# Conditioned hybrid decoder layer on one core: the last gate's modulation in two runs, the expert weights' parts in another buffer, the ending shared by three engines

## The chip, the cores and the metric

The kernel runs on one core of a Trainium2 chip. The metric is the device time of one launch in microseconds (us). A profile is one further execution, recorded instruction by instruction; its times are counted from the start of its span.

## The reference, cut to what matters

Everything is float32. A prompt of 256 tokens and 8 sample sequences of 4 tokens (together T = 288 token columns, TP = 256 and TS = 32) pass through one layer. The layer's conditioning gives six modulation vectors per sequence; the last is `gate2`.

```
shift1, scale1, gate1, shift2, scale2, gate2 = split(silu(c) @ w_ada + b_ada)
h = rms_norm(x) * (1 + scale1) + shift1
... projections, sparse attention, conformer convolution, merge ...
x = x + gate1 * (merged @ w_out)
h2 = rms_norm(x) * (1 + scale2) + shift2
x = x + gate2 * peer(h2)

def peer(h):                      # 16384 experts, a row of u_emb and of v_emb each
    q = h @ w_q_peer              # 8 heads, two halves of 128
    pick 16 experts per head and token, softmax gates
    act = gelu(u_emb[picked] . h)
    return sum(gate * act * v_emb[picked])
```

## The kernel before, in words

The expert tables are not gathered for the prompt. All 16384 experts are computed densely in NSUB = 128 chunks of 128 experts: first `scores` for every chunk (u_emb chunk times h2, then gelu, stored to DRAM), later `outputs` for every chunk (v_emb chunk times the gated activations, summed in the eight PSUM banks `ps0` to `ps7`, one for each 128 output features). Only the 32 sample tokens gather their rows of v_emb, by indirect DMAs on POOL. To keep float32 accuracy at the speed of the rounded format, every weight tile and every right-hand side is cut into a high and a low part: ScalarE (ACT) copies the high part, POOL or VectorE (DVE) subtracts it for the low part, and TensorE (PE) multiplies high by high, high by low and low by high.

There is no scheduler. Each engine has its own instruction list, written out by hand or in hardware loops (`Fori`), and the lists are tied by counting semaphores (`wait_ge`). Each engine works its list strictly in order. SyncE (SP) issues the loads of the weight tiles into a ring of R = 4 slots.

Three places matter here.

**The last gate's modulation.** The tiles of w_ada for `gate2` come late. PE runs `late_ada(i, s, j)` for i in 0, 1: four float32 matmuls of 32x128 output each. It stands where PE would otherwise wait: behind the sums of squares of the second RMSNorm (`sums`, L1770), while ACT takes the root (L777), DVE the reciprocal (L1505), and h2 is made (DVE L1513, ACT L999 for the high part, DVE L1516 and L1520 for the low part). The half with i = 0 has two filler matmuls (`keep_busy`, L2120) behind each call; the half with i = 1 stands between the eight high-by-high matmuls of the first tile of the expert queries (`linear_cut(("peer_q", 0))`: L1832 high by high, L1842 high by low, L1848 low by high).

**From the last scores to the first outputs.** `scores` is L2171, L2172 and L2178 on PE, gelu is L1065 on ACT, the cut of a tile L1009 on ACT. The gated activations of a chunk are themselves cut: ACT L1103 makes the high part, DVE L1678 the low part, in a buffer `wr` that lies over the right-hand side of `scores`:

```
wr = rhs_parts[:, :, :]...            # the right-hand side of scores
...
eng.wait_ge(u_done, NSUB)             # ACT, ahead of the first high part of wr
...
pe.wait_ge(gelued, NSUB)              # PE, ahead of the first outputs
```

`outputs` is L2228 (high tile by both parts of `wr`, 512 columns) and L2231 (low tile by high part). DVE L1684 makes the low part of a v_emb tile.

**The ending.** The last `outputs` finishes the banks one after the other (`bank_done`). DVE adds `gate2` times the two halves of each bank to x: `first_half` (L1739) and `second_half` (L1744) for k = 0 to 7. Behind bank 4 PE multiplies the summed rows of the sample tokens (`samples`, L2256), which must wait until bank 0 has been read (`y_out` of 1) since they go into it; DVE scales and adds them (L1754, L1759). SP stores y in two DMAs of four chunks each (L638).

## Time and profile before

| | |
|---|---|
| median of 3 runs | 1251.37 us (1250.25 to 1252.94) |
| the profiled execution | 1250.7 us |
| its span | 1248.9 us |
| mean granted TensorE clock | 0.995 |
| PE busy | 1207.5 us (97% of the span) |
| DVE busy | 921.9 us (74%) |
| ACT busy | 592.2 us (47%) |
| POOL busy | 616.6 us (49%) |

Busy time of PE is modelled, since matmuls are pipelined: overlapping matmuls count once. PEld is the weight load of a matmul, which runs beside the matmul before it. Idle time of an engine that nobody waits for costs nothing. The profiled execution took 1.8 us more than its span, which lies outside of what the records show.

### The profile page before, as it was taken

To read this page: it belongs to the slowest core of one execution; us is meant where nothing else is said; L and a number is where in the kernel's file an instruction comes from. 1 tells how busy PE (TensorE), PEld (TensorE's weight loads), DVE (VectorE), ACT (ScalarE), POOL (GpSimd) and SP (SyncE) were. 2 spreads that over 40 slices of the span, in tenths; PEclk is the share of its full clock that TensorE was granted. 3 is DMA by queue.
4 is the path that set the end of the run, shared out by engine and by line. 5 is a ranking of instruction groups with operands and counts; after the bars stand their busy time and mean duration, and the time that the engine had idled before them with its cause. 6 is when DMAs were issued, how large, how long until landed. Compare 5 with 4: busy or idle time off the path is not lost.

```text
span 1248.9 us, 28196 instructions
## 1 busy us (share of the span) xinstructions
PE 1207.5 (97%) x8837; PEld 1114.8 (89%) x8837; DVE 921.9 (74%) x2247; ACT 592.2 (47%) x1015; POOL 616.6 (49%) x307
## 2 busy tenths in 40 slices
PE   5999999989999999999999999999999999999997
PEld 3887877989979999999999999999888888888886
DVE  4779985966754999959999998000567888888866
ACT  2332445657443445445554545444455455554452
POOL 0664564521755667766666666777203434434100
PEclk9999999999999999999999999999999999999999
DMA  9986555423743356655555555667767898888763
GB/s 361 318 268 223 166 199 186 140 86 120 262 151 135 125 188 207 214 186 188 185 180 183 182 179 186 205 207 246 255 232 284 308 345 290 309 310 309 275 225 125
DMA packets 113995, 273.12 MB, mean 219 GB/s; under 512 B 30928, under 2 KB 54192, under 8 KB 113552
## 3 DMA queue, kind: packets, MB, share of 16 engines
q1 hardware_dynamic: 105920, 248.96, 58.7%
q0 software_dynamic: 6432, 19.71, 4.4%
q10 hardware_dynamic: 1584, 3.68, 0.8%
q8 instruction: 34, 0.56, 0.2%
q14 instruction: 25, 0.20, 0.1%
HBM read 249.30 MB, written 23.00 MB: 218 GB/s over the span
## 4 chain that ended last, share of the span: by engine, by line
PE 82%; DVE 10%; DMA 2%; issue 1%; SPq 1%; ACT 1%; POOL 1%; ACTq 0%; DVEq 0%; POOLq 0%
PE ps L2228 19%; PE ps L2171 11%; PE ps L2178 11%; PE ps L2172 11%; PE ps L2231 10%; DVE ps L1212 6%; PE ps L1832 5%; PE ps L1848 5%; PE ps L1842 5%; PE ps L2207 2%; DMA ring<-in_stream 2%; DVE big L1231 1%; DVE big L1228 1%; PE ps L2148 1%; SPq L557 1%
## 5 line engine op out<-in xcount | busy, mean ns | idle before, releaser
L728 POOL TENSOR_TENSOR split<-ring,split 128x1024 fp32r<-128x1024 f32 x128 | 307.4, 2402 | 138.6 <-ACT split L1009 138.6
L1009 ACT ACTIVATE split<-ring 128x1024 fp32r<-128x1024 f32 x256 | 271.6, 1061 | 174.5 <-PE ps L2228 171.5
L668 POOL TENSOR_TENSOR split<-ring,split 128x1024 fp32r<-128x1024 f32 x76 | 186.8, 2463 | 190.5 <-ACT split L828 190.5
L2171 PE MATMUL ps<-h2r,split 128*128 128x288 f32 x1024 | 278.7, 297 | 0.7 <-ACT big L1035 0.5
L2172 PE MATMUL ps<-h2r,split 128*128 128x288 f32 x1024 | 279.0, 296 | 0.0
L2228 PE MATMUL ps<-h2r,split 128*128 128x512 f32 x1024 | 257.4, 392 | 1.4 <-DVE h2r L1678 1.4
L2228 PEld LDWEIGHTS ps<-h2r,split 128*128 128x128 f32 x1024 | 184.2, 189 | 34.5 <-issue 1.6
L2171 PEld LDWEIGHTS ps<-h2r,split 128*128 128x128 f32 x1024 | 192.9, 188 | 1.2 <-ACT big L1035 0.8
L2172 PEld LDWEIGHTS ps<-h2r,split 128*128 128x128 f32 x1024 | 192.4, 188 | 0.0
L2178 PE MATMUL ps<-h2r,split 128*128 128x288 f32 x1024 | 156.5, 295 | 0.0
L1684 DVE TENSOR_TENSOR split<-ring,split 128x1024 fp32r<-128x1024 f32 x128 | 156.1, 1219 | 0.0
L1065 ACT ACTIVATE act<-ps 128x288 f32<-128x288 f32 x124 | 51.0, 412 | 219.4 <-PE ps L2178 216.5
L741 POOL DMA_INDIRECT big<-in_stream,pick_at x32 | 62.8, 1962 | 175.6 <-DVE big L1698 127.9
L2231 PEld LDWEIGHTS ps<-h2r,split 128*128 128x128 f32 x1024 | 140.0, 190 | 9.9
L2231 PE MATMUL ps<-h2r,split 128*128 128x256 f32 x1024 | 143.8, 282 | 0.0
L2178 PEld LDWEIGHTS ps<-h2r,split 128*128 128x128 f32 x1024 | 141.4, 188 | 0.3 <-POOL split L728 0.3
L1637 DVE SCALAR_TENSOR_TENSOR hot<-ps,parts 128x256 fp32r<-128x256 f32 x256 | 124.2, 485 | 0.0
L828 ACT ACTIVATE split<-ring 128x1024 fp32r<-128x1024 f32 x84 | 88.6, 1055 | 62.9 <-DMA ring<-in_stream 52.0
L1212 DVE SCALAR_TENSOR_TENSOR ps<-big,ps 128x256 f32<-128x256 f32 x232 | 97.1, 485 | 2.0
L1636 DVE TENSOR_SCALAR hot<-ps,parts 128x128 fp32r<-128x128 f32 x256 | 90.0, 352 | 11.2 <-PE ps L2207 11.2
L1832 PE MATMUL ps<-h2r,split 128*128 128x288 f32 x544 | 89.8, 306 | 3.8 <-ACT split L828 3.7
L1832 PEld LDWEIGHTS ps<-h2r,split 128*128 128x128 f32 x544 | 76.5, 190 | 14.7 <-issue 9.7
(290 smaller groups left out, 1619.8 us busy)
## 6 DMA issues: line engine op xcount, KB each, us to landing
ring<-in_stream SPq DMA_DIRECT2D x371, 512.0 KB
act_dram<-act SPq DMA_DIRECT2D x128, 128.0 KB, 1.8
big<-in_stream SPq DMA_DIRECT2D x20, 512.0 KB, 7.6
parts<-act_dram SPq DMA_DIRECT2D x16, 512.0 KB
big<-act_dram SPq DMA_DIRECT2D x16, 512.0 KB, 5.2
big<-in_cache_k SPq DMA_DIRECT2D x16, 128.0 KB, 2.6
big<-in_cache_v SPq DMA_DIRECT2D x16, 128.0 KB, 3.0
s_act_dram<-act SPq DMA_DIRECT2D x128, 16.0 KB, 1.5
```

Of the source, the lines that this page charges most:

```text
L668: nc.gpsimd.tensor_tensor(split[:, n % 2, 1], ring[:, POS[CUT[n]] % R, :], split[:, n % 2, 0].bitcast(f32), ALU.subtract).then_inc(lin_lo, 1)
L728: nc.gpsimd.tensor_tensor(split[:, n % 2, 1], ring[:, slot_of(n), :], split[:, n % 2, 0].bitcast(f32), ALU.subtract).then_inc(lo_ready, 1)
L1009: nc.scalar.activation(split[:, n % 2, 0], ring[:, slot_of(n), :], ACT.Copy).then_inc(hi_ready, 1)
L1212: ins = V.scalar_tensor_tensor(acc if j < CW - 1 else y[:, k, 0:TP], zp[:, k, j:j + TP], w, acc, ALU.mult, ALU.add)
L1637: return V.scalar_tensor_tensor(hot1[:, slot], iota_ps.unsqueeze(1).to_broadcast([P, 2, P]), parts[:, 0, col], parts[:, 2:4, col].to_broad ...
L1684: V.tensor_tensor(split[:, n % 2, 1], ring[:, slot_of(n), :], split[:, n % 2, 0].bitcast(f32), ALU.subtract).then_inc(lo_ready, 1)
L1832: MM(out, hi[:, k], rhs_h[:, k], start=(k == 0), stop=False)
L2171: MM(out, u_hi[:, k], h_hi[:, k], start=(k == 0), stop=False)
L2172: last = MM(out, u_hi[:, k], h_lo[:, k], start=False, stop=False)
L2178: last = MM(out, u_lo[:, k], h_hi[:, k], start=False, stop=(k == KC - 1))
L2228: return MM(ps[k][:, 0:2 * TP], v[0][:, k], w_both, start=first, stop=last)
L2231: return MM(ps[k][:, 0:TP], v[1][:, k], wr[:, n % 2, 0], start=False, stop=False)
```

## The change

It does three things, and none of them changes what is computed.

1. The two halves of `late_ada` run one behind the other with four fillers between them, ahead of the first tile of the expert queries, whose matmuls stand alone again.
2. `wr` lies over the one-hot rows (`hot1`), which are no longer used by then. So ACT makes the first high part behind the third last chunk's place in the gelu list, `behind` the gelu of chunk 126, and PE starts the first outputs with banks 2 to 7; it waits for the last gelu only ahead of banks 0 and 1, which the scores used. DVE's first low tile waits for the last scores where it waited for those before.
3. At the end the second halves of k = 1, 3 and 5 are scaled by ACT into `y_low` and added by POOL, and the sample tokens' tail is copied out of PSUM by ACT and scaled and added by POOL. DVE waits for ACT to have read a shared bank before it reads it. SP stores y in five DMAs: four of two chunks' prompt columns, and one of all sample columns.

```diff
-        wr = rhs_parts[:, :, :].rearrange("p a n -> p (a n)")[:, 0:4 * TP].rearrange("p (s a t) -> p s a t", a=2, t=TP)
+        wr = hot1[:, :, :, :].rearrange("p n a i -> p (n a i)").rearrange("p (s a t) -> p s a t", a=2, t=TP)
+        SHARED = (1, 3, 5)
+        y_low = parts[:, 0:len(SHARED)]
@@ sync
-            sp.wait_ge(s_scaled, 2)
-            for half in range(2):
-                ks = slice(half * KC // 2, (half + 1) * KC // 2)
-                sp.wait_ge(y_out, ks.stop)
-                sp.dma_start(a["yT"][:, ks], ye[:, ks]).then_inc(stored, 16)
-            sp.wait_ge(stored, 16 * 6)
+            for k in range(0, KC, 2):
+                sp.wait_ge(y_out, sum(n not in SHARED for n in range(k + 2)))
+                sp.wait_ge(y_odd, sum(n < k + 2 for n in SHARED))
+                if k == KC - 2:
+                    sp.wait_ge(s_scaled, 2)
+                    sp.dma_start(a["yT"][:, :, TP:T], ye[:, :, TP:T]).then_inc(stored, 16)
+                sp.dma_start(a["yT"][:, k:k + 2, 0:TP], ye[:, k:k + 2, 0:TP]).then_inc(stored, 16)
+            sp.wait_ge(stored, 16 * 9)
@@ gpsimd, at its end
+            pool.wait_ge(x_loaded, 16)
+            for i, k in enumerate(SHARED):
+                pool.wait_ge(y_scaled, i + 1)
+                pool.wait_ge(y_half, k + 1)
+                nc.gpsimd.tensor_tensor(ye[:, k, 0:TP], ye[:, k, 0:TP], y_low[:, i], ALU.add).then_inc(y_odd, 1)
+                if i == 1:
+                    pool.wait_ge(s_unfolded, 1)
+                    picked = dtmp.rearrange("p (k b t) -> p k b t", b=NSEQ, t=TD)
+                    nc.gpsimd.tensor_tensor(picked, picked, gate2[:, :, 1:NG].unsqueeze(3).to_broadcast([P, KC, NSEQ, TD]),
+                                            ALU.mult).then_inc(s_scaled, 1)
+                    pool.wait_ge(s_scaled, 1)
+                    nc.gpsimd.tensor_tensor(ye[:, :, TP:T], dtmp.rearrange("p (k c) -> p k c", c=TS), xe[:, :, TP:T],
+                                            ALU.add).then_inc(s_scaled, 1)
@@ scalar
-            with eng.Fori((BEFORE + MIXED) // R, NSUB // R) as g:
+            with eng.Fori((BEFORE + MIXED) // R, NSUB // R - 1) as g:
                 turn(g, False)
+            def high_weights(g, b, n, first=False):
+                eng.wait_ge(weighted, g * R + (n + 1))
+                if not first:
+                    eng.wait_ge(o_done, g * R + (n - 1))
+                nc.scalar.activation(wr[:, n % 2, 0], act_bs[b][:, n], ACT.Copy).then_inc(w_hi, 1)
+            turn(NSUB // R - 1, False, lambda: high_weights(0, 0, 0, True), R - 2)
...
+            for i, k in enumerate(SHARED):
+                eng.wait_ge(bank_done, k + 1)
+                nc.scalar.activation(y_low[:, i], ps[k][:, TP:2 * TP], ACT.Copy, scale=gate2[:, k, 0:1]).then_inc(y_scaled, 1)
+                if i == 1:
+                    eng.wait_ge(s_folded, 1)
+                    nc.scalar.activation(dtmp, ps[0][:, 0:KC * TS], ACT.Copy).then_inc(s_unfolded, 1)
@@ vector
-                    value_low(c, n, *((u_done, NSUB - 1 + i) if first and i < 2 else (o_done, c - 1)))
+                    value_low(c, n, *((u_done, NSUB) if first and i < 2 else (o_done, c - 1)))
...
                 if k + 1 < KC:
+                    if k + 1 in SHARED:
+                        dve.wait_ge(y_scaled, SHARED.index(k + 1) + 1)
                     first_half(k + 1)
-                second_half(k)
-                if k == 4:
-                    dve.wait_ge(s_folded, 1)
...
+                if k not in SHARED:
+                    second_half(k)
@@ tensor
-            for s in range(R):
-                for j in range(2):
-                    late_ada(0, s, j)
-                    keep_busy(2)
+            for i in range(2):
+                for s in range(R):
+                    for j in range(2):
+                        late_ada(i, s, j)
+                if i == 0:
+                    keep_busy(4)
...
-                linear_cut(("peer_q", n), between=(lambda k: late_ada(1, k // 2, k % 2)) if n == 0 else None)
+                linear_cut(("peer_q", n))
...
-                for k in range(KC):
+                for k in (*range(2, KC), 0, 1) if first else range(KC):
+                    if first and k == 0:
+                        pe.wait_ge(gelued, NSUB)
                     ins = high(k)
...
-            pe.wait_ge(gelued, NSUB)
```

On PE, from the sums of squares (L1770) into the first expert query tile. `ps5` and `ps6` take the two halves of the modulation, `ps7` the fillers, `ps0` the query tile. Before:

```order
L1770 MATMUL ps3<-big,ones 128x288 x2
L1875 MATMUL ps5<-big 32x128 x4
L2120 MATMUL ps7<-y_r 128x288 x2
L1875 MATMUL ps5<-big 32x128 x4
L2120 MATMUL ps7<-y_r 128x288 x2
...
L1832 MATMUL ps0<-h2r,split 128x288
L1875 MATMUL ps6<-big 32x128 x4
L1832 MATMUL ps0<-h2r,split 128x288
L1875 MATMUL ps6<-big 32x128 x4
...
L1842 MATMUL ps0<-h2r,split 128x288 x8
L1848 MATMUL ps0<-h2r,split 128x288 x8
```

And in the changed kernel, where the same functions stand at L1803 (`sums`), L1906 (`late_ada`), L2151 (filler) and L1865, L1873, L1879 (the three products):

```order
L2151 MATMUL ps7<-y_r 128x288 x6
L1803 MATMUL ps3<-big,ones 128x288 x2
L1906 MATMUL ps5<-big 32x128 x32
L2151 MATMUL ps7<-y_r 128x288 x4
L1906 MATMUL ps6<-big 32x128 x32
L1865 MATMUL ps0<-h2r,split 128x288 x8
L1873 MATMUL ps0<-h2r,split 128x288 x8
L1879 MATMUL ps0<-h2r,split 128x288 x8
```

The second half has moved ahead of the query tile, and 12 of 16 fillers are gone.

On ACT of the changed kernel, the last four chunks' gelus (L1089), the cuts of tiles (L1033) and the high parts of `wr` (L1126), which before all stood behind the last gelu:

```order
L1033 ACTIVATE split<-ring 128x1024
L1089 ACTIVATE act<-ps0 128x288
L1126 ACTIVATE hot1<-parts 128x256
L1033 ACTIVATE split<-ring 128x1024
L1089 ACTIVATE act<-ps1 128x288
L1033 ACTIVATE split<-ring 128x1024
L1126 ACTIVATE hot1<-parts 128x256
```

The first high part stands ahead of the cut of tile 128 and of the last gelu; the second stands where it stood.

On DVE at the very end, before (L1739 is a first half, L1744 a second half, `psN` the bank):

```order
L1739 SCALAR_TENSOR_TENSOR big<-ps0,gate2,big 128x256
L1739 SCALAR_TENSOR_TENSOR big<-ps1,gate2,big 128x256
L1744 SCALAR_TENSOR_TENSOR big<-ps0,gate2,big 128x256
...
L1739 SCALAR_TENSOR_TENSOR big<-ps5,gate2,big 128x256
L1744 SCALAR_TENSOR_TENSOR big<-ps4,gate2,big 128x256
L1754 TENSOR_TENSOR big<-ps0,gate2 128x256
L1759 TENSOR_TENSOR big<-big 128x8x32
L1739 SCALAR_TENSOR_TENSOR big<-ps6,gate2,big 128x256
L1744 SCALAR_TENSOR_TENSOR big<-ps5,gate2,big 128x256
L1739 SCALAR_TENSOR_TENSOR big<-ps7,gate2,big 128x256
L1744 SCALAR_TENSOR_TENSOR big<-ps6,gate2,big 128x256
L1744 SCALAR_TENSOR_TENSOR big<-ps7,gate2,big 128x256
```

And in the changed kernel (L1777 a first half, L1782 a second half):

```order
L1777 SCALAR_TENSOR_TENSOR big<-ps0,gate2,big 128x256
L1777 SCALAR_TENSOR_TENSOR big<-ps1,gate2,big 128x256
L1782 SCALAR_TENSOR_TENSOR big<-ps0,gate2,big 128x256
...
L1777 SCALAR_TENSOR_TENSOR big<-ps4,gate2,big 128x256
L1777 SCALAR_TENSOR_TENSOR big<-ps5,gate2,big 128x256
L1782 SCALAR_TENSOR_TENSOR big<-ps4,gate2,big 128x256
L1777 SCALAR_TENSOR_TENSOR big<-ps6,gate2,big 128x256
L1777 SCALAR_TENSOR_TENSOR big<-ps7,gate2,big 128x256
L1782 SCALAR_TENSOR_TENSOR big<-ps6,gate2,big 128x256
L1782 SCALAR_TENSOR_TENSOR big<-ps7,gate2,big 128x256
```

Three second halves and the two instructions of the sample tokens are gone from the list; the first halves of `ps1`, `ps3` and `ps5` each wait for ACT.

## Rows read from the trace of the kernel before

**Rows 1.** The page: busy time, share of the span, instructions by engine.

```profile
PE 1207.5 (97%) x8837; PEld 1114.8 (89%) x8837; DVE 921.9 (74%) x2247; ACT 592.2 (47%) x1015; POOL 616.6 (49%) x307
```

**Rows 2.** Waits of PE from 377 to 1243, largest first: us, times, longest.

```profile
PE ps L2148 <- ACT big L818: 2.0, 4, 0.5
PE ps L2228 <- DVE h2r L1678: 1.4, 1, 1.4
...
```

**Rows 3.** Timeline around the modulation: start, length, instruction, idle before it.

```profile
361.95 1.21 PE L1770 MATMUL ps<-big,ones 128*128 128x288 f32 x4 [0.69 <-DVE big L1492]
363.08 0.43 PE L1875 MATMUL ps<-big 128*32 128x128 f32 x8
367.03 3.31 ACT L999 ACTIVATE h2r<-big,mod 128x256 fp32r<-128x256 f32 x8
...
369.99 3.25 DVE L1520 SCALAR_TENSOR_TENSOR h2r<-big,mod,h2r 128x256 fp32r<-128x256 f32 x8
376.07 1.22 PE L1848 MATMUL ps<-h2r,split 128*128 128x288 f32 x8
```

**Rows 4.** Timeline: long runs of the same 32-wide matmuls early in the kernel.

```profile
16.54 3.64 PE L1864 MATMUL ps<-big 128*32 128x128 f32 x64
21.11 1.52 PE L1864 MATMUL ps<-big 128*32 128x128 f32 x48
```

**Rows 5.** Stretches, PE alone: length, PE busy (matmuls), granted clock, DMA share, GB/s.

```profile
178.00:181.40 3.40, 1.95 (x14) 0.99 0.89 292
181.50:184.50 3.00, 3.00 (x14) 0.50 0.03 11
369.40:374.90 5.50, 5.50 (x74) 1.00 0.00 1
```

**Rows 6.** Timeline from the last scores to the first outputs.

```profile
881.43 0.41 ACT L1065 ACTIVATE act<-ps 128x288 f32<-128x288 f32 x1 [1.76 <-PE ps L2178]
881.74 0.41 ACT L1103 ACTIVATE h2r<-parts 128x256 fp32r<-128x256 f32 x1
882.18 0.43 DVE L1678 TENSOR_TENSOR h2r<-parts,h2r 128x256 fp32r<-128x256 f32 x1 [18.93 <-ACT h2r L1103]
882.75 2.06 PE L2228 MATMUL ps<-h2r,split 128*128 128x512 f32 x8 [1.36 <-DVE h2r L1678]
882.85 1.22 DVE L1684 TENSOR_TENSOR split<-ring,split 128x1024 fp32r<-128x1024 f32 x1
890.49 1.06 ACT L1009 ACTIVATE split<-ring 128x1024 fp32r<-128x1024 f32 x1 [1.41 <-DMA ring<-in_stream]
893.98 2.00 PE L2228 MATMUL ps<-h2r,split 128*128 128x512 f32 x8
```

**Rows 7.** Timeline of the ending.

```profile
1238.19 0.88 DVE L1739 SCALAR_TENSOR_TENSOR big<-ps,gate,big 128x256 f32<-128x256 f32 x2 [1.14 <-PE ps L2228]
1239.60 1.94 PE L2256 MATMUL ps<-fold,big 128*128 128x32 f32 x16
...
1242.02 0.48 DVE L1739 SCALAR_TENSOR_TENSOR big<-ps,gate,big 128x256 f32<-128x256 f32 x1 [0.21 <-PE ps L2228]
...
1244.78 0.87 DVE L1744 SCALAR_TENSOR_TENSOR big<-ps,gate,big 128x256 f32<-128x256 f32 x2
1245.67 0.35 SPq L638 DMA_DIRECT2D out_yT<-big  x1
```

**Rows 8.** Nearest rows for the new operations; DMAs: KB each, us to landing.

```profile
L682 POOL TENSOR_TENSOR big<-big 128x256 f32<-128x256 f32 x7 | 5.2, 739 | 0.8 <-POOL big L682 0.5
L1040 ACT ACTIVATE big<-ps 128x256 f32<-128x256 f32 x1 | 0.4, 383 | 0.0
act_dram<-act SPq DMA_DIRECT2D x128, 128.0 KB, 1.8
s_act_dram<-act SPq DMA_DIRECT2D x128, 16.0 KB, 1.5
out_yT<-big SPq DMA_DIRECT2D x2, 576.0 KB, 2.8
```

More of the change, by code:

```diff
@@ L425, in build @@
         y_half = sem("y_half")
+        y_scaled = sem("y_scaled")
+        y_odd = sem("y_odd")
+        s_unfolded = sem("s_unfolded")
         s_scaled = sem("s_scaled")
@@ L1055, in _, with turn @@
                 gelu(c, c, c < 2)
-            def turn(g, tokens4, behind_first=None):
+            def turn(g, tokens4, behind=None, at=0):
                 for n in range(R):
@@ L1065, in turn @@
                     nc.scalar.activation(act[:, n % 2], ps[n % 2][:, 0:T], ACT.Gelu_apprx_tanh).then_inc(gelued, 1)
-                    if behind_first and n == 0:
-                        behind_first()
+                    if behind and n == at:
+                        behind()
                     if tokens4:
@@ L1093, in _ @@
                 turn(g, True)
-            with eng.Fori((BEFORE + MIXED) // R, NSUB // R) as g:
+            with eng.Fori((BEFORE + MIXED) // R, NSUB // R - 1) as g:
                 turn(g, False)
+            def high_weights(g, b, n, first=False):
[4 more added lines that the diff above has]
+            turn(NSUB // R - 1, False, lambda: high_weights(0, 0, 0, True), R - 2)
             def v_turn(g, b, first=False, last=False):
                 for n in range(R):
-                    eng.wait_ge(weighted, g * R + (n + 1))
-                    if not first or n >= 2:
-                        eng.wait_ge(o_done, g * R + (n - 1))
-                    nc.scalar.activation(wr[:, n % 2, 0], act_bs[b][:, n], ACT.Copy).then_inc(w_hi, 1)
+                    if not first or n:
+                        high_weights(g, b, n, first and n < 2)
                     m = (n + 1) % R
@@ L1749, in _ @@
                 if k + 1 < KC:
+                    if k + 1 in SHARED:
+                        dve.wait_ge(y_scaled, SHARED.index(k + 1) + 1)
                     first_half(k + 1)
-                second_half(k)
-                if k == 4:
-                    dve.wait_ge(s_folded, 1)
-                    V.tensor_tensor(dtmp.rearrange("p (k b t) -> p k b t", b=NSEQ, t=TD),
-                                    ps[0][:, 0:KC * TS].rearrange("p (k b t) -> p k b t", b=NSEQ, t=TD),
-                                    gate2[:, :, 1:NG].unsqueeze(3).to_broadcast([P, KC, NSEQ, TD]), ALU.mult)\
-                        .then_inc(s_scaled, 1)
-                    dve.wait_ge(s_scaled, 1)
-                    V.tensor_tensor(ye[:, :, TP:T], dtmp.rearrange("p (k c) -> p k c", c=TS), xe[:, :, TP:T], ALU.add)\
-                        .then_inc(s_scaled, 1)
+                if k not in SHARED:
+                    second_half(k)
         @block.tensor
@@ L1812, in _, with linear_cut @@
             g_hi, g_lo = (rhs_other[:, part].rearrange("p (k t) -> p k t", t=T) for part in range(2))
-            def linear_cut(key, *halves, between=None):
+            def linear_cut(key, *halves):
                 n = CUT.index(key)
@@ L1832, in linear_cut @@
                             MM(out, hi[:, k], rhs_h[:, k], start=(k == 0), stop=False)
-                            if between:
-                                between(k)
                     if key == ("peer_q", 0) and half == 0:
```

## The prediction

> **What bounds the kernel now.** I read the profile's page first: PE is busy 97% of the span, every other engine 74% or less [rows 1]. Then all waits of PE from 377 us to the ending: four of 0.5 us in which it waits for ACT's copy of a query tile (L2148), and one of 1.4 us ahead of the first outputs; what is left out is shorter still [rows 2]. So between 377 and 1243 us nothing but PE's own work takes time: if PE gets to 377 earlier, the end comes earlier by as much. The places where PE doesn't work at full density are those that the change touches: the thin stretch before 377 us, the 1.4 us before the first outputs, and the ending, where DVE and a store come last. I read the timeline of the three, one after the other.
>
> **Part 1, the modulation.** It adds no work and takes 12 fillers away. What matters is which chain lets the third product of the first query tile (low by high) start, and at what time. It starts at 376.07 and takes 1.22 [rows 3]. Behind the sums, which end at 361.95 + 1.21 = 363.16, PE now has 32 float32 matmuls, four fillers, 32 matmuls. In the trace a float32 matmul shows as two rows, so each run is 64 rows. 48 such rows took 1.52 us, which makes 2.0 for 64; another run of 64 took 3.64 [rows 4]. Fillers go by the dense 128x288 matmul, 1.22 / 8 = 0.15 each [rows 3]. PE reaches the query tile at 363.16 + 2.0 + 0.6 + 2.0 = 367.8 at the best, at 371.0 at the worst. There it meets two chains that don't change: ACT makes the eight high pieces of h2 from 367.03, the last at 370.34; DVE makes the low pieces from 369.99, the last at 369.99 + 3.25 = 373.24 [rows 3]. Even from 371.0, eight high-by-high matmuls are done at 372.2. So DVE comes last in both cases, and the low-by-high product starts at about 373.4 instead of 376.07: **−2.6 us**. Before, PE reached that point later than DVE, because eight late_ada calls stood between. The cuts and copies behind this tile (ACT, POOL) were released by PE and move along.
>
> What it gives back is the clock. From 367.8 to 373.4 PE has 16 matmuls of 0.15, that is 2.4 us of work in 5.6 us. The interleaved calls kept it busy for 5.50 of 5.50 us there, at a granted clock of 1.00 [rows 5]. Elsewhere, after a stretch of 3.40 us with 1.95 busy, the clock stood at 0.50 for the next 3.00 us [rows 5], the 1.2 GHz level. If it falls here, a stretch of such length costs at most half of it, 1.5 us, if it lies wholly in the dense work behind 373.4, and nothing if it lies wholly in the thin part. It should reach over both; I take **+1.0** of 0 to 1.5. (TensorE: Matmul & The Clock Gate of the Trainium skill, section "Why this matters for your kernels", warns of idle gaps between bursts. The gaps here are of 0.25 us between single matmuls, so by that rule there would be no fall and the term would be 0; the row at 178 us holds a gap of its own, so it doesn't tell the two apart.)
>
> **Part 2, the first outputs.** PE is free at 882.75 − 1.36 = 881.39, and waits for a chain that began with the last gelu: gelu 881.43, first high part 881.74, first low part 882.18 [rows 6]. Now the high part is made one gelu earlier and the low part follows on DVE, which had been idle for 18.93 us [rows 6]. Bank 0 waits for the last gelu, done at 881.84, but is now the seventh bank in the list, and each takes 2.06 / 8 = 0.26, so it is wanted 1.5 us after the start. The high tile by bank 2 can start at once. The DVE low part of the tile, 1.22 us from 882.85 before [rows 6], only waits for the last scores, so it comes at about 881.4 to 882.7, before the low-by-high product needs it at 881.4 + 2.1 = 883.5. I take the whole wait, **−1.4**. The lower bound of the gain is set further on. The tile whose cut ACT began at 890.49 was waited for as a transfer, and that transfer isn't made earlier, since SP issues it after a store that hangs on the last gelu. The cut ends at 891.55, the parts of the weights follow it (0.40 on ACT, 0.43 on DVE: 892.4), and PE used them at 893.98; now it wants them at 892.6 [rows 6]. That leaves 0.2 us. If the transfer or a neighbour slips by more, it eats the gain one for one. So 0 to 1.4.
>
> **Part 3, the ending.** DVE's list loses three second halves and two operations of the sample tokens, at about 0.4 us each. But the first half of bank 1 now waits for ACT's read of it: 0.38 [rows 8]. Two first halves took 0.88 from 1238.19 [rows 7], so the second started at about 1238.6; now 1239.0. The reading of bank 0 and so the sample matmuls slip from 1239.60 to about 1239.95, and bank 5 from 1242.02 to 1242.4 [rows 7]. ACT copies the folded samples first, then scales bank 5: the first half of 5 starts at about 1242.8. Behind it stand five halves 0.40 apart, the last 0.48 long: 1245.3, against 1244.78 + 0.87 = 1245.65 [rows 7]. POOL takes 0.74 for an operation of this size [rows 8]. Three of them from 1242.2 end at 1244.4, hidden by DVE with 0.8 to spare. SP then issues the sample columns and, 0.4 later, the last pair, at about 1245.7, no earlier than the last store before (1245.67, landing 2.8 later with 576 KB [rows 7, 8]). The last is 256 KB now; 128 KB landed after 1.8 [rows 8]. Between the two by size is 2.1; with three more stores close by I take 2.4. **−0.4**, of −0.7 to +0.8, the upper end if DVE's list or POOL's is longer by two operations.
>
> The term that no row shows is the store of the sample columns: 1024 rows of 128 B. The nearest is the store of 16 KB in rows of 128 B, which landed after 1.5, where 128 KB in rows of 1 KB took 1.8 [rows 8]. Small rows were not dear there, but there were only 8 for each of the 16 DMA engines; here there are 64. Below: 1.8, as for its size. Above: if all of the 1.5 us were row time, 64/8 x 1.5 = 12. I take it as hidden in the last store's 2.4. (DMA: Bandwidth & Descriptors of the Trainium skill, section "Specifications", wants 512 B or more for the line rate and has a read-modify-write below that, which speaks against this store; the pair of rows neither shows nor excludes it at this count.)
>
> **Sum.** −2.6 + 1.0 − 1.4 − 0.4 = −3.4. The profiled execution took 1250.7, 0.67 less than the median of the three runs, 1251.37. So 1247.3 for a run like the profiled one, and **1247.9** as median.
>
> **Rivals.**
> - **No fall of the clock** (22%). For: the matmuls never stop for longer than a fraction of a us. Against: the row at 0.50 after a stretch of similar density. 1246.9. (This is where the Trainium skill's rule on idle gaps, named above, would lead.)
> - **The wait before the first outputs comes back later** (10%), at the tile cut at 890.49, with 0.2 us of slack. Part 2 is worth nothing: 1249.3.
> - **The ending costs** (10%). ACT stands ahead of DVE three times, and each wait may be longer than the 0.38; POOL's three operations may be slower. +0.6 for −0.4: 1248.9.
> - **Part 1 pays nothing** (8%). The clock falls for longer, or more than once, or PE's first tile waits for something else at its new place, such as the low part of the next tile. 1250.5.
> - **Slower: the store of the sample columns** (6%). It is issued at about 1245.3, and all stores were landed at 1248.47 before. Without the ending the change gives −3.0, so it breaks even when that store takes 1248.47 + 3.0 − 1245.3 = 6.2 us, or 96 ns for a row on each engine. At the ceiling of 12 us the end is at 1257.3, 8.8 later than before: 1251.4 + 8.8 − 3.0 = 1257.2.
> - What is left, 44%, is the forecast, its own range 1247.2 to 1248.9.
>
> **How the numbers follow.** This kernel's runs lie 2.7 us apart, so I call 0.2% (2.5 us, 1248.9) the least that can be told from no change. Faster: the forecast less its upper edge (42%), no fall (22%), half of the costly ending (5%), together about 0.69. Same: the returned wait (10%), part 1 for nothing (8%), the other half of the ending (5%), and the edge (2%): 0.25. Slower: 0.06. The range goes from 1246.2 (no fall, and the ending at −0.7, less some scatter) to 1250.5; above it lie the slow rival and a part of the rival ahead, under 2 in 10 together.
>
> **What would show it.** In the profile after: low by high (L1879) of the first query tile starts within 0.3 us of 373.4, right behind DVE's last low piece; the granted clock between 371 and 377 tells forecast from first rival. No idle before the first L2261, and none behind it that names a DMA or ACT near 892. DVE's first half of bank 5 waits for ACT and the last second half ends near 1245.3 minus what PE gained; the last two stores land within 3 us of their issue. A PE that waits for POOL at the second query tile, a cut near 890 that still waits for its transfer while PE waits for the cut, or a store of the samples that lands after the last pair would each make it wrong.

## The result, and the profile after

The changed kernel takes 1254.96 us (median of 10 runs, 1252.68 to 1257.52), the kernel before 1250.28 in the 10 runs beside it. The ratio is 1.0032, 95% interval 1.002 to 1.0045: slower by about 4 us, where 3.4 less was forecast. The profiled execution took 1255.31 us, its span 1253.4.

The page of the changed kernel: busy time by engine, and the granted clock in 40 slices.

```profile
PE 1212.0 (97%) x8825; PEld 1117.6 (89%) x8825; DVE 917.5 (73%) x2242; ACT 595.3 (47%) x1019; POOL 605.1 (48%) x312
PEclk9999999899999999999999999999999999999998
```

PE is still busy 97% of the time, and 12 matmuls fewer take 4.5 us more than in [rows 1]. A page alone doesn't tell why. What does is to cut both traces at the same five events and to compare the stretches:

| stretch, us | before | after | difference |
|---|---|---|---|
| start to the first matmul of the second norm's sums | 361.95 | 363.25 | +1.30 |
| from there to the second query tile | 15.18 | 13.54 | −1.64 |
| to the first scores | 61.91 | 61.90 | −0.01 |
| to the first outputs | 443.71 | 442.19 | −1.52 |
| to DVE's first read of bank 0 | 355.44 | 359.70 | +4.26 |
| to the end of the span | 10.71 | 12.84 | +2.13 |

DVE's first read of bank 0 is the first `first_half`, where the ending begins. The first line lies ahead of the change and is taken up with the experiments. The second and fourth are parts 1 and 2 of the prediction, near what it said. The fifth and the sixth are the loss.

**The modulation.** Timeline of the changed kernel (start, length, instruction, idle before it), and PE in stretches (length, busy, granted clock, DMA share, GB/s):

```profile
363.25 1.21 PE L1803 MATMUL ps<-big,ones 128*128 128x288 f32 x4 [0.68 <-DVE big L1530]
364.39 1.95 PE L1906 MATMUL ps<-big 128*32 128x128 f32 x64
366.27 0.79 PE L2151 MATMUL ps<-y_r 128*128 128x288 f32 x4
366.99 1.96 PE L1906 MATMUL ps<-big 128*32 128x128 f32 x64
368.99 3.10 PE L1865 MATMUL ps<-h2r,split 128*128 128x288 f32 x8
...
371.29 3.25 DVE L1558 SCALAR_TENSOR_TENSOR h2r<-big,mod,h2r 128x256 fp32r<-128x256 f32 x8
...
375.01 1.95 PE L1879 MATMUL ps<-h2r,split 128*128 128x288 f32 x8
376.79 1.22 PE L1865 MATMUL ps<-h2r,split 128*128 128x288 f32 x8
```

```profile
371.40:373.20 1.80, 1.80 (x6) 1.00 0.02 5
373.20:376.60 3.40, 3.40 (x12) 0.50 0.02 5
376.60:380.00 3.40, 3.40 (x28) 1.00 0.46 154
```

Both runs of 64 rows took 1.96 us, and low by high starts 11.76 us behind the sums' first matmul, 14.12 before [rows 3]. In the second half of the thin stretch the clock falls to 1.2 GHz, and the eight matmuls from 375.01 take 1.95 us for 1.22.

**The first outputs.** In the changed kernel PE goes from the last scores to the first outputs without idle time (the wait of 1.36 us in [rows 6] is gone):

```profile
879.81 1.23 PE L2211 MATMUL ps<-h2r,split 128*128 128x288 f32 x8
880.88 2.02 PE L2261 MATMUL ps<-hot,split 128*128 128x512 f32 x8
```

**The outputs.** Both kernels at the same place, 120 us into the outputs. Before:

```profile
1000.13 2.00 PE L2228 MATMUL ps<-h2r,split 128*128 128x512 f32 x8
1001.97 1.11 PE L2231 MATMUL ps<-h2r,split 128*128 128x256 f32 x8
1002.92 0.86 PE L2228 MATMUL ps<-h2r,split 128*128 128x512 f32 x3
```

After:

```profile
999.69 2.03 PE L2261 MATMUL ps<-hot,split 128*128 128x512 f32 x8
1001.55 1.12 PE L2264 MATMUL ps<-hot,split 128*128 128x256 f32 x8
1002.51 0.86 PE L2261 MATMUL ps<-hot,split 128*128 128x512 f32 x3
```

The sixteen matmuls of a chunk are called a group here: eight 128x512 of the high tile (the high product) and eight 128x256 of the low tile (the low product). The starts are to be read, not the lengths: from one group to the next it is 2.79 us before and 2.82 after. Over all groups the medians are 2.793 and 2.827; from the sixth on they scatter by about 1 ns (standard deviation). PE waits for nobody in either once the first group has started. 126 intervals at 0.034 make the 4.3 us. The only thing that changed in these matmuls is where `wr` lies.

**The ending.** The changed kernel:

```profile
1240.58 0.48 DVE L1777 SCALAR_TENSOR_TENSOR big<-ps,gate,big 128x256 f32<-128x256 f32 x1 [1.18 <-PE ps L2261]
...
1241.37 0.48 DVE L1777 SCALAR_TENSOR_TENSOR big<-ps,gate,big 128x256 f32<-128x256 f32 x1 [0.31 <-ACT parts L1151]
...
1245.32 0.48 DVE L1777 SCALAR_TENSOR_TENSOR big<-ps,gate,big 128x256 f32<-128x256 f32 x1 [1.51 <-ACT parts L1151]
...
1246.24 0.73 POOL L781 TENSOR_TENSOR big<-big,parts 128x256 f32<-128x256 f32 x1
1246.89 0.87 DVE L1782 SCALAR_TENSOR_TENSOR big<-ps,gate,big 128x256 f32<-128x256 f32 x2
1247.79 0.60 SPq L647 DMA_DIRECT2D out_yT<-big  x1
1248.44 0.65 SPq L648 DMA_DIRECT2D out_yT<-big  x1
```

DVE is done 7.18 us behind its first read of bank 0 (7.46 before, [rows 7]), the stores landed at 1251.18 by the raw records, and the span ends at 1253.4. In the raw records each engine closes the program with a `DRAIN`, which no view lists, and the one that ends last is POOL's; the span ends 0.24 us behind it. Its records (start us, length ns):

```
before   POOL DRAIN 1163.206 11817     last landing 1248.50   span 1248.89
after    POOL DRAIN 1245.915  7265     last landing 1251.18   span 1253.42
```

### The profile page after: what moved, and what is told of

It reads as the page before. It is cut to its first block, busy times and chain, and to the rows that moved or that the text cites. A ratio compares the mean times of both kernels' runs of the same rounds, so it can differ in the third digit from the quotient of the medians.

```text
span 1253.4 us, 28179 instructions
## 1 busy us (share of the span) xinstructions
PE 1212.0 (97%) x8825; PEld 1117.6 (89%) x8825; DVE 917.5 (73%) x2242; ACT 595.3 (47%) x1019; POOL 605.1 (48%) x312
## 4 chain that ended last, share of the span: by engine, by line
PE 83%; DVE 10%; DMA 3%; issue 1%; SPq 1%; ACT 1%; POOL 1%; DVEq 0%; ACTq 0%; POOLq 0%
PE ps L2261 19%; PE ps L2204 11%; PE ps L2211 11%; PE ps L2205 11%; PE ps L2264 10%; DVE ps L1250 6%; PE ps L1865 5%; PE ps L1879 5%; PE ps L1873 5%; DMA ring<-in_stream 3%; PE ps L2240 2%; DVE big L1269 1%; DVE big L1266 1%; PE ps L2181 1%; SPq L564 1%
## 5 line engine op out<-in xcount | busy, mean ns | idle before, releaser
L1033 ACT ACTIVATE split<-ring 128x1024 fp32r<-128x1024 f32 x256 | 271.4, 1060 | 176.5 <-PE ps L2261 168.4
L2261 PE MATMUL ps<-hot,split 128*128 128x512 f32 x1024 | 260.6, 395 | 0.0
L2261 PEld LDWEIGHTS ps<-hot,split 128*128 128x128 f32 x1024 | 183.7, 188 | 35.1
L2204 PEld LDWEIGHTS ps<-h2r,split 128*128 128x128 f32 x1024 | 192.9, 188 | 1.2 <-ACT big L1059 0.8
L2205 PEld LDWEIGHTS ps<-h2r,split 128*128 128x128 f32 x1024 | 192.5, 188 | 0.0
L1089 ACT ACTIVATE act<-ps 128x288 f32<-128x288 f32 x124 | 51.2, 413 | 219.1 <-PE ps L2211 216.4
L2264 PEld LDWEIGHTS ps<-hot,split 128*128 128x128 f32 x1024 | 140.6, 188 | 11.7
L751 POOL DMA_INDIRECT big<-in_stream,pick_at x32 | 52.7, 1646 | 190.3 <-DVE big L1736 143.6
L2264 PE MATMUL ps<-hot,split 128*128 128x256 f32 x1024 | 144.5, 282 | 0.0
L2211 PEld LDWEIGHTS ps<-h2r,split 128*128 128x128 f32 x1024 | 141.5, 188 | 0.3 <-POOL split L738 0.3
L1865 PE MATMUL ps<-h2r,split 128*128 128x288 f32 x544 | 90.7, 308 | 3.1 <-ACT split L852 2.9
L1865 PEld LDWEIGHTS ps<-h2r,split 128*128 128x128 f32 x544 | 77.3, 192 | 14.4 <-issue 7.4
```

The source lines that it names most:

```text
L1033: nc.scalar.activation(split[:, n % 2, 0], ring[:, slot_of(n), :], ACT.Copy).then_inc(hi_ready, 1)
L1865: MM(out, hi[:, k], rhs_h[:, k], start=(k == 0), stop=False)
L2204: MM(out, u_hi[:, k], h_hi[:, k], start=(k == 0), stop=False)
L2205: last = MM(out, u_hi[:, k], h_lo[:, k], start=False, stop=False)
L2211: last = MM(out, u_lo[:, k], h_hi[:, k], start=False, stop=(k == KC - 1))
L2261: return MM(ps[k][:, 0:2 * TP], v[0][:, k], w_both, start=first, stop=last)
```

## The experiments

One table holds all figures: the stretches of each profiled execution (us), and the ratio of its timed runs to those of the kernel before on the same chip. From the second query tile to the first scores all took 61.9 or 62.0 (e3 62.7, since its clock was still at half when the second tile began).

| run | to the sums | to query tile 2 | scores | outputs | ending | ratio [95%] |
|---|---|---|---|---|---|---|
| before | 361.95 | 15.18 | 443.71 | 355.44 | 10.71 | |
| after | 363.25 | 13.54 | 442.19 | 359.70 | 12.84 | 1.0032 [1.002, 1.0045] |
| e1 | 362.12 | 13.67 | 439.67 | 357.70 | 12.83 | 1.0003 [0.9986, 1.002] |
| e2 | 359.39 | 15.18 | 443.69 | 356.29 | 10.70 | 1.001 [0.9995, 1.0024] |
| e3 | 360.28 | 13.68 | 442.53 | 361.35 | 10.67 | 1.0015 [1.0, 1.0029] |
| e4 | 359.93 | 15.19 | 443.72 | 355.46 | 14.06 | 1.0044 [1.0029, 1.006] |
| e5 | 364.79 | 13.60 | 443.73 | 355.44 | 10.69 | 0.9999 [0.999, 1.0008] |
| e6 | 359.57 | 15.19 | 443.73 | 356.00 | 10.70 | one run |
| e7 | 359.62 | 15.18 | 443.69 | 358.85 | 10.70 | one run |
| e8 | 361.39 | 12.77 | 439.69 | 355.43 | 10.67 | 0.9961 [0.9948, 0.9975] |
| e9 | 364.06 | 12.77 | 443.77 | 355.45 | 10.69 | 0.9975 [0.9961, 0.999] |
| e10 | 365.13 | 15.20 | 443.71 | 355.45 | 11.27 | one run |
| e11 | 363.32 | 15.20 | 439.67 | 355.43 | 10.67 | 0.9967 [0.9954, 0.998] |
| e12 | 361.11 | 12.79 | 439.67 | 355.43 | 10.22 | 0.9942 [0.9921, 0.9963] |
| e13 | 361.52 | 13.66 | 441.81 | 357.47 | 12.85 | 1.0005 [0.9992, 1.0019] |
| e14 | 361.17 | 12.77 | 439.70 | 354.59 | 10.21 | 0.9945 [0.9932, 0.9959] |

**e1: `hot1` on a multiple of 64.** In both kernels `hot1` starts at byte 221920 of a partition, the old `wr` at 49280.

```diff
+        sb("pad", 8)
         hot1 = sb("hot1", NHOT, 2, P, dt=f32r)
```

> The changed kernel with eight unused words (32 bytes) ahead of hot1, so that wr starts at byte 221952 of a partition, a multiple of 64, and not at 221920, which is 32 past one. Nothing else. Theory 'start': the high tile's 128x512 product of the outputs reads wr in pieces of 64 bytes, and a start off such a piece costs one more piece for each matmul; the trace of the changed kernel has 2.83 us from one group of eight to the next in the outputs, before had 2.79. It expects 2.79 again, 4.3 us less over the 127 groups, so about 1250.7 by the changed kernel's median of 1255.0; perhaps 1 us less still, since the one-hot matmuls read hot1 too. Rival 'neighbour': hot1 is slower because it lies close to parts and the other small buffers that ACT and DVE write at the same time. It expects 2.83 and no change, 1255. Rival 'order': the outputs are slower since the weights' parts are made one step earlier; no change either.

The time came as expected, the stretches did not. The outputs gained 2.0, not 4.3: the two slots of `wr` take 2.821 and 2.799 us for a group, and two groups near 887, where ACT's cut waited for a transfer, were 0.1 longer. The scores gained 2.5, not 1. All of it lies in the part in which the one-hot matmuls run (231.14 us, 233.63 in the changed kernel); they read `hot1` and `hot2`, which the unused words both shift. A right total from two wrong terms; the start matters, but not in units of 64 bytes alone.

**e2: the kernel before with `wr` 32 bytes on.**

```diff
-... [:, 0:4 * TP].rearrange("p (s a t) -> p s a t", a=2, t=TP)
+... [:, 8:8 + 4 * TP].rearrange("p (s a t) -> p s a t", a=2, t=TP)
```

> The kernel before with one edit: wr starts 8 words (32 bytes) further into the right-hand side's buffer, so 32 bytes past a multiple of 64, and is read and written as before. Theory 'start': 2.83 us for each group of the outputs in place of 2.79, so about +4.3 us on the kernel before (ratio 1.0034), with the buffer, its neighbours and the order of before. Rivals 'neighbour' and 'order': no change, ratio 1.000.

A miss in size: 2.800 us for a group, +0.85 us in the outputs. The high product went from 1.841 to 1.867 as in the changed kernel, but the low one from 0.953 to 0.933. So a start alone changes both products, in either direction, and the first form of the theory (one more piece of 64 bytes) falls.

**e3: the changed kernel with the ending of before** (DVE, ACT, POOL and SP lists of the ending as before).

> The changed kernel with the ending of before: all halves and the sample tokens on DVE, nothing on ACT and POOL, two stores. From the first read of bank 0 to the end of the span the trace has 10.7 us before and 12.8 after. Theory 'drain': what closes the program on POOL (a drain of 7.3 us that the raw records show from 1245.9 to 1253.2 in the changed kernel, 6.2 us past POOL's last addition, and that lay hidden at 1163 to 1175 before) ends after all else. It expects 10.7 from bank 0 to the end again, and about 2.1 us less than the changed kernel: 1252.9. Rival 'stores': the five stores cost the 2.1 us; it expects the same here, and is told apart by e4. Rival of the prediction's sum: the shared ending saves, so taking it out costs 0.4: 1255.4.

The ending is 10.67 us again, and the median 1252.84. But other stretches of its profile differ too. The clock was at half for 6.8 us, so that the first part of the change gained 0.7 us up to the scores and not 1.6:

```profile
368.80:375.60 6.80, 6.80 (x24) 0.50 0.08 21
```

The outputs took 361.35, 1.65 more than in the changed kernel with the same `wr`. PE waited once, near 890, for the chain that starts with the load of a tile (us, times, longest):

```profile
PE ps L2242 <- DVE hot L1692: 1.5, 1, 1.5
```

**e4: the kernel before with a late instruction on POOL.**

```diff
                 gather_score(j)
+
+            pool.wait_ge(y_out, KC)
+            nc.gpsimd.memset(parts[:, 0, 0:4], 0.0)
```

> The kernel before with one added instruction on POOL: it waits until all eight banks are added on DVE (1245.65 in the trace before) and writes 4 words of a buffer that is no longer read. Nothing waits for it. Theory 'drain': POOL's closing then begins at about 1246 and takes 6 to 7 us past the added instruction, so the span ends at 1252.0 to 1252.6 and not at 1248.9: +3.1 to +3.7 us, ratio 1.0025 to 1.003. Rival 'stores' or any other in which POOL's closing costs nothing: the stores still end last, at 1248.5, and nothing changes.

Timeline of its last instructions:

```profile
1242.81 0.86 DVE L1747 SCALAR_TENSOR_TENSOR big<-ps,gate,big 128x256 f32<-128x256 f32 x2
1243.70 0.35 SPq L638 DMA_DIRECT2D out_yT<-big  x1
1243.73 0.10 POOL L768 MEMSET parts<- 128x4 f32 x1 [78.41 <-DVE big L1747]
```

Nobody waits for these 0.10 us, and the span ends 6.4 us behind them: POOL's `DRAIN` runs from 1243.71 for 6.32 us, the stores had landed at 1246.51. The ending is 3.35 us longer. The timed runs lose 0.29% to 0.6%, somewhat more than the trace's 0.27%.

**e5: the first part of the change alone**, on the kernel before.

> The kernel before with the first part of the change alone: both halves of the last gate's modulation in two runs with four fillers between, the first query tile's matmuls alone. The changed kernel and two variants of it all show the granted clock at half somewhere between 368 and 376 us. If the prediction's part 1 holds: low by high of the first query tile starts 11.8 us after the sums' first matmul (14.1 before), the clock falls to 0.50 for 3.4 us, and the second query tile starts 1.6 us earlier against the sums than before, so -1.6 us (ratio 0.9987). Rival 'no fall': -2.4. Rival 'pays nothing': 0. The outputs stay at 2.793 us for a group and the ending at 10.7.

The stretch and the fall came as forecast (0.50 from 374.9 to 378.3), −1.58 us. But the timed runs are equal to before, 0.9999, and 0.9987 lies just outside the interval. That asked for e9.

**e6 and e7: four starts in one run.** The kernel before, with `wr` in four slots. The edit of e6 is shown, with its starts in words; e7 has (24, 32, 152, 160):

```diff
+        WR = (0, 8, 4, 12)
+        flat = rhs_parts[:, :, :].rearrange("p a n -> p (a n)")
+        wrs = [flat[:, s * 4 * TP + o:s * 4 * TP + o + 2 * TP].rearrange("p (a t) -> p a t", t=TP) for s, o in enumerate(WR)]
```

> The kernel before with four slots for wr in place of two, one for each chunk of a group of four, each 4096 bytes on and with a start of its own: 0, 32, 16 and 48 bytes past a multiple of 64. So one run shows the time of a group of outputs matmuls at four starts. Theory 'start' in its first form (a piece of 64 bytes more): slot 0 as before, 2.793 us and 1.84 for its eight 128x512 matmuls, the other three alike, near 1.87. If it is the address in more bits than these, the pattern of the eight gaps within slot 1 is that of e2 (234 231 235 233 ns) only where its higher bits don't matter. Rival 'neighbour': all four alike at 2.793.

> As the run before, with starts 96, 128, 608 and 640 bytes past those of the kernel before (which is 128 past a multiple of 512). Slot 0 then agrees with the changed kernel's wr in the low nine bits of its address, slot 2 in the low twelve; slots 1 and 3 agree so with the wr of e1. Theory 'start': slots 0 and 2 take 2.827 and show the changed kernel's pattern of gaps in the high product (238 231 232 ns, repeated), slots 1 and 3 take about 2.80 to 2.82. Rival 'neighbour': wr lies in the old buffer, so all take 2.793.

Mean gaps between matmul starts over all 30 groups of a slot, worked out from the traces (ns; start of `wr` modulo 512 bytes; high and low are the sums over eight gaps):

```
run, slot      start  group  high  low    the eight gaps of the low product
before            128   2793  1841   952   113 119 120 120 120 120 120 120
e6 slot 0         128   2795  1846   949   117 118 119 121 117 118 120 120
e6 slot 2         144   2787  1853   933   114 119 114 119 114 119 114 119
e2, both          160   2800  1867   933   116 117 117 116 117 117 116 117
e6 slot 1         160   2803  1870   933   117 117 117 117 117 117 117 117
e6 slot 3         176   2802  1857   944   118 117 116 118 120 117 120 118
after, both       224   2827  1867   959   118 121 117 125 116 123 118 121
e7 slots 0, 2     224   2832  1873   959   118 121 117 125 116 124 118 121
e7 slots 1, 3     256   2808  1855   953   117 123 120 119 115 118 121 120
e1 slot 0         256   2821  1867   954   122 120 119 115 117 122 120 119
e1 slot 1         256   2799  1857   942   118 113 116 124 120 119 115 117
e13, both         128   2793  1841   953   114 119 120 120 120 120 120 120
e14, both         144   2787  1853   933   119 114 119 114 119 114 119 114
```

In e7 `wr` lies in the old buffer, written and read as before, and the outputs take 3.41 us more than before. Slots 0 and 2 have the changed kernel's gaps in the low product to 1 ns; in the high product the expected pattern did not come (227 236 233 235 232 240 233 237, where the changed kernel has 237 231 232 repeated), and a group takes 5 ns more. Slots 0 and 2 start 512 bytes apart (and two slots of 4096), as slots 1 and 3 do, and agree to the nanosecond. So the move to another buffer is not needed for the cost: the start counts, in bits below 512.

It is not all. The same start gives 2793 or 2795, 2800 or 2803 and 2827 or 2832, the second of each in a run whose other slots start elsewhere; that the slot ahead does it is a guess. And the two slots of e1 differ by 22 at one start. The weights' tile alternates between two places as the slots do. Where both slots have the same start (128, 144, 160 and 224) that makes no difference, at 256 in e1 it may; no run separates the two.

**e8: a candidate.** The changed kernel with `hot1` as in e1, the ending of before, `wr` over `hot1` for the first four chunks alone, a filler behind each matmul of the first two products of the first query tile, and SP's wait for the stored activations behind the first four loads of v_emb tiles:

```diff
+        def wr_of(c):
+            return wr_first if isinstance(c, int) and c < R else wr_later
...
+                            if key == ("peer_q", 0):
+                                keep_busy(1)
...
-            for s in range(2):
-                sp.wait_ge(act_stored[s], 32 * NSUB // 2)
...
             for n in range(R):
                 load_expert(NSUB + n, n)
+            for s in range(2):
+                sp.wait_ge(act_stored[s], 32 * NSUB // 2)
```

> A candidate that keeps what pays: the changed kernel with hot1 on a multiple of 64; wr over hot1 for the first four chunks alone and where it was before for the other 124; the ending of before; a filler behind each of the sixteen matmuls of the first query tile's first two products, to hold the clock; and SP's wait for the stored activations behind the first four loads of v_emb tiles, not ahead of them. By the traces so far, against before: modulation -2.4 (-1.6 if the clock falls in spite of the fillers), first outputs -1.4 and no wait for a tile between 885 and 893, one-hot products on an aligned buffer -2.3 (first outputs 503.6 us behind the first query tile's last product in e1, 505.9 in the changed kernel), outputs 2.793 for a group, ending 10.7. Sum -6.1: ratio 0.995. If the early loads collide with the stores that they now overtake, a wait comes back near 890 and it is -5.

0.9961, 1245.0 us against 1249.89. Its stretches are as expected (−6.5 us in sum where −6.1 was); the timed ratio says −4.9. Near 883 ACT now waits for PE and no longer for a transfer, and with the fillers the clock stays up (two views of e8):

```profile
883.48 1.06 ACT L1020 ACTIVATE split<-ring 128x1024 fp32r<-128x1024 f32 x1 [1.43 <-PE ps L2250]
```

```profile
367.10:369.50 2.40, 2.37 (x13) 1.00 0.00 0
369.50:374.80 5.30, 5.30 (x34) 1.00 0.02 5
```

**e9: the modulation with fillers, on the kernel before.**

> The kernel before with the first part of the change alone, and one filler behind each of the sixteen matmuls of the first query tile's first two products. The trace of the candidate shows that with them the clock stays up and the second query tile starts 12.8 us after the sums' first matmul (13.6 without fillers in e5, 15.2 before). If what lies between the sums and the end were all, this would be -2.4 us (ratio 0.998). e5 was timed equal to before (0.9999) where its stretch behind the sums gained 1.6. In all five traces with the new modulation the clock fell near 28 us, in the five without it once, and their sums start at 362.4 on average against 360.1. Theory 'start-up': something in the first 80 us is dearer in these programs by 1.5 to 2.5 us: then the ratio is 0.999 to 1.000 here too. Rival 'chance': the profiles fell so by chance, ratio 0.998.

0.9975, by its stretch 0.9981. So the modulation pays, and 'start-up' gets little support.

**e10: the kernel before with five stores.**

> The kernel before with its ending on DVE as it was, but y stored as in the changed kernel: four stores of two chunks' prompt columns and, ahead of the last, one of all sample columns in 1024 rows of 128 bytes. In the changed kernel the stores landed 3.4 us after DVE's last half (1247.76 to 1251.18), before 2.85 (1245.65 to 1248.50). If the stores cost what that says, the span's part from the first read of bank 0 is 11.3 here, against 10.7; the store of the sample columns takes 0.6 to issue and about 1.1 to move. The prediction's slower rival (96 ns and more for a row on each engine) expects 13 and more; its sum expects 10.3.

The ending is 11.27, 0.56 longer, as the changed kernel said. Rows of its end:

```profile
1248.00 0.87 DVE L1745 SCALAR_TENSOR_TENSOR big<-ps,gate,big 128x256 f32<-128x256 f32 x2
1248.90 0.60 SPq L638 DMA_DIRECT2D out_yT<-big  x1
1249.54 0.66 SPq L639 DMA_DIRECT2D out_yT<-big  x1
```

**e11: the candidate with the old modulation.**

> The candidate e8 with the modulation of before. By the traces its stretches are: first outputs -1.5 and one-hot products -2.5 in the scores, all else as before, so -4.0 us (ratio 0.9968). e8 was timed at 0.9961 where its stretches said -6.4 (0.9949). Theory 'start-up': the new modulation costs 1.5 to 2.5 us ahead of the sums, so that it gives 1 us at most in all, and this kernel comes out within 1 us of e8 (0.996 to 0.997). Rival 'chance': e8 is 2.4 us faster than this one.

0.9967, just what its own stretches say (−4.07 us). e10 and e11 have the old modulation and still come to the sums at 365.1 and 363.3, with the clock at half for 6.8 us from 27.5 and 25.7. So what differs ahead of the sums is not tied to the new modulation, and 'start-up' is dropped. Against e8 the ratio differs by 0.0006 where the stretches say 0.002; the intervals overlap and don't decide that.

**e12: the candidate with three stores** (four chunks, two and two, full rows).

```diff
+            for lo, end_k in ((0, 4), (4, 6), (6, 8)):
+                ks = slice(lo, end_k)
```

> The candidate e8 with y stored in three pieces of full rows, four chunks, two and two, so that the last store is 288 KB and not 576. In the trace of before the last store's rows move from about 1247.0 to 1248.2; with half of them that is about 0.6 to 0.8 less. Expected: 9.9 to 10.1 us from the first read of bank 0 to the end of the span, 10.7 before, and a ratio of 0.9955 (e8: 0.9961). If a store's length is mostly the time until its first row, the ending stays at 10.5 or more.

10.22, 0.45 less than e8, where 0.6 to 0.8 was forecast. At 0.9942 (1243.12 us against 1250.22) it is the fastest by median ratio.

**e13: `hot1` at the old start modulo 512.** The edit of e1 with 104 words in place of 8.

> The changed kernel with 104 unused words (416 bytes) ahead of hot1, so that wr starts at byte 222336, which is 128 past a multiple of 512, as the wr of the kernel before (49280) is. In e7, starts that agree in their low nine bits gave the same time in every slot, so theory 'low nine bits' expects here what before had, in the changed kernel's own buffer: 2.793 us for a group of outputs and 1.841 for its high product (233 236 228 232 231 227 227 227 ns), 355.5 us for the stretch of the outputs in place of 359.7, so 4.2 less than the changed kernel; and 1 to 2.5 us less in the scores, since the one-hot rows start there too. Against before: modulation -1.6, scores -4, outputs 0, ending +2.1: ratio 0.997. Rival 'buffer': e1, whose wr starts at 256 past a multiple of 512, had 2.821 and 2.799 in its two slots where e7 had 2.808 in the old buffer, so something of the buffer may matter as well; then 2.80 to 2.82 here. Early waits for tiles near 890 may add up to 1.5 in either case.

2.793 us for a group and the gaps of before to 1 ns, in the changed kernel's own buffer: this settles the fifth stretch. The total was a miss, 1.0005 where 0.997 was forecast. The one-hot matmuls gain only 0.4 at this start, and PE, now faster, waits for a tile's transfer as in e3 (the wait, and ACT's cut that was late):

```profile
PE ps L2262 <- DVE hot L1717: 1.8, 1, 1.8
```

```profile
890.14 1.06 ACT L1034 ACTIVATE split<-ring 128x1024 fp32r<-128x1024 f32 x1 [5.01 <-DMA ring<-in_stream]
```

**e14: e12 with the later `wr` 16 bytes on.**

> The candidate with three stores (e12) with wr for the chunks from the fifth on starting 4 words later, 144 bytes past a multiple of 512. Slot 2 of e6 had this start and took 2.787 us for a group, the start of before 2.793 to 2.795. If the start alone sets it, 123 groups by 6 to 8 ns make 0.7 to 1.0 us less in the stretch of the outputs: 354.5 in place of 355.4, a ratio 0.0007 below that of e12, which timing alone can't tell but the trace can. If it is the start together with that of the weights' tile (slot 2 has the same one as slot 0) then slot 1 of this kernel, which goes with the other weights' tile, is slower and the gain is half or none.

2.787 us for a group in both slots, 354.59 in the outputs, 0.84 less than e12. In the timed runs (0.9945) this can't be seen.

## Why the prediction was wrong

**What bounds the kernel.** Right: PE passes every shift on. That is also why 34 ns in each of 126 intervals came through whole.

**Part 1** was right in mechanism and size. −2.6 was forecast for the start of low by high, −2.4 came; +1.0 for the clock, and +0.7 came (1.95 for 1.22 us). −1.6 in sum, as forecast; in e3, where the clock stayed down for 6.8 us, it was −0.7. PE came to the query tile 5.74 us behind the sums (5.85 forecast). The rival without a fall is refuted: the clock fell in each of the five traces with this part and no fillers (the changed kernel, e1, e3, e5, e13), and in none of the four with fillers (e8, e9, e12, e14). The Trainium skill (TensorE: Matmul & The Clock Gate, "Why this matters for your kernels") warns of idle gaps between bursts; here the matmuls of the thin stretch started at most 0.40 us apart, and the clock fell, so this trace does not agree with that rule taken alone.

**Part 2** gained −1.5 (−1.4 forecast) up to the first outputs. Its lower bound was well placed: in e3 and e13 the same edit lost 1.5 and 1.8 us again at the tile near 890, named in the prediction with 0.2 us of slack. The changed kernel lost only 0.1 there in its profiled execution, with the same groups as e3: it hangs on when the last stores land, since SP's loads wait for them: the loads were issued at 887.02 in the changed kernel, 6.1 us behind the first outputs, and 7.0 and 7.4 behind them in e3 and e13. With SP's early loads (e8, e11, e12, e14) nothing was lost.

**The step that failed first** is what the prediction didn't price. It followed who writes and reads `wr` and when, took PE's own work between 377 and 1243 us as given, and so each of the 2048 matmuls of the outputs to last as before; its sum has no term for them. Moving `wr` to a start of 224 modulo 512 costs 4.26 us in the fifth stretch. e7 shows a cost (+3.41) without the move, e13 the move without the cost. By which rule the bits act stays open, and with it the two slots of e1: the low product is faster at 144 and 160 than at 128, the high one slower. The Trainium skill (SBUF — State Buffer, "Operand start alignment") lets a float32 operand start at any multiple of 4 bytes and says that this is about legality, not speed; the runs show the speed.

**The step that failed second** is the end of part 3, forecast −0.4, measured +2.13. DVE's list was nearly right (7.18 us, 7.11 forecast; −0.28 against before). The stores landed 3.42 us behind DVE's last half, 2.85 before: +0.57, of which e10 shows 0.56 alone. The last store is issued 0.68 us behind DVE's end where it was 0.02, since the issue of the sample columns stands ahead of it (0.60 long, 0.4 in the prediction), and lands 2.74 behind its own issue, not 2.4. And the sum took the last landing for the end of the program: POOL's closing adds 1.85 (1253.42 − 1251.18 = 2.24, where 0.39 lay before). e3 takes it away, e4 makes it alone. The prediction had POOL's three operations "hidden by DVE with 0.8 to spare"; they were, and POOL's own end was not.

**The slower rival**, the store of sample columns at 96 ns and more for a row, was the wrong one. By the raw records its rows take 13 ns each and move in 1.05 us. Two stretches of the changed kernel (the last two figures are DMA share and GB/s) hold small rows alone and rows of the last pair alone:

```profile
1249.20:1249.80 0.60, 0.00 (x0) 0.50 0.94 146
1250.10:1250.50 0.40, 0.00 (x0) 0.50 0.99 353
```

The Trainium skill (DMA: Bandwidth & Descriptors, "Specifications"), which speaks against rows below 512 B, agrees in direction: 146 GB/s against 353. The price was small all the same, since only 128 KB go that way.

**A slip in the rivals.** 'Part 1 pays nothing' was given as 1250.5. The forecast of 1247.9 without part 1's −1.6 is 1249.5; 1250.5 keeps the +1.0 of the clock and drops the gain. The measured 1254.96 lies above either.

**Ahead of the sums** the two profiles differ by 1.30 us, which e10 and e11 show not to be tied to the new modulation. The runs of one kernel lie as far apart (1252.68 to 1257.52), so one profile of each can't say more; the timed ratio, +2.5 to +5.6 us, fits the other stretches, +3.2. Open remains e5, timed 1.5 us slower than its stretch says, and e4, timed slower than its trace.

## What to carry to other kernels

An operand's start address is part of a change that moves a buffer: work out old and new start modulo 512, and if the matmuls that read it are the bound, compare the gap between their starts, since busy time hides a difference of 2 or 3 ns for a matmul. Give an engine no last work near the end of the program before knowing how long its closing takes; the last landing is not the end. And a gain that makes the bounding engine arrive earlier should be paid for in advance, by loads that don't wait for what they don't need.

## What the runs showed of the hardware

- The time of a 128x512 or 128x256 matmul depends on the start of its moving operand in SBUF, in bits below 512: a chunk's sixteen took 2.787 to 2.832 us at six starts, the same within about 1 ns from group to group of a slot. One step of 16 bytes was worth 0.84 us in the whole (e14).
- POOL's closing `DRAIN` ends some 6.2 us behind POOL's last instruction (6.22 in the changed kernel, 6.20 in e4), whether that is an addition of 0.73 us or a write of 0.10. Those of DVE, ACT and PE end 0.05, 0.04 and 0.05 us behind theirs in the changed kernel.
- While PE's 128x288 matmuls of 0.15 us started up to 0.40 us apart, with no long gap, its clock fell to 1.2 GHz, for 3.4 us in four traces and 6.8 in one (e3); one 128x288 filler behind each matmul prevented it in four of four and delayed nothing (low by high 11.72 us behind the sums, 11.76 without).
